# Products without a reader in TensorE's two waits ahead of the expert stage of a hybrid decoder layer

## The reference

```
h = RMSNorm(x + mixers(x))                      # two token mixers ahead of this
g = argmax over 4 groups of h @ w_router_group + b
e1, e2 = the two largest of the 8 experts of group g
combine = softmax weight of the group x softmax over the two experts
y = sum over the two experts of (silu(h @ w_gate[e]) * (h @ w_up[e]) * combine) @ w_down[e]
out = RMSNorm(x + mixers(x) + y)
```

## Time and profile before

| | us |
|---|---|
| median of three runs | 734.78 |
| lowest and highest run | 734.08, 737.99 |
| span of the profiled execution, first to last instruction | 733.4 |
| TensorE's mean granted clock in it, share of full speed | 0.950 |

### The profile page before, as it was taken

One profiled execution on the slowest core, in us unless ns is written; L12 is line 12 of the kernel. 1 busy time (PEld: TensorE's weight loads), 2 busy tenths in 40 slices (PEclk: granted clock), 3 DMA queues, 4 the chain that ended last, 5 costly groups with the idle time before them and its releaser, 6 DMA issues.

```text
span 733.4 us, 13507 instructions
## 1 busy us (share of the span) xinstructions
PE 637.2 (87%) x4935; PEld 450.3 (61%) x4935; DVE 281.4 (38%) x1551; ACT 149.3 (20%) x425; POOL 103.4 (14%) x137
## 2 busy tenths in 40 slices
PE   6999999799999989999998999638997995768674
PEld 4888888687888767743535877436653554444431
DVE  3003845988878976400000222535233221110103
ACT  3333323233326222200010000211100110101013
POOL 1456206320100324000000000011100110000001
PEclk9999999999999999999999999858998998999996
DMA  9938997999998999769999699668999999999871
GB/s 308 291 116 296 365 370 251 328 352 381 348 337 311 391 351 363 301 246 349 410 409 360 224 423 388 266 214 311 351 391 402 372 389 397 388 390 416 365 264 61
DMA packets 94901, 242.86 MB, mean 331 GB/s; under 512 B 8834, under 2 KB 54530, under 8 KB 86514
## 3 DMA queue, kind: packets, MB, share of 16 engines
q1 hardware_dynamic: 58050, 193.51, 69.9%
q10 hardware_dynamic: 31200, 31.39, 12.9%
q0 software_dynamic: 5584, 17.08, 6.9%
HBM read 234.88 MB, written 9.11 MB: 333 GB/s over the span
## 4 chain that ended last, share of the span: by engine, by line
PE 65%; DMA 19%; DVE 9%; SPq 3%; issue 2%; ACT 1%; ACTq 0%; DVEq 0%; POOLq 0%
PE zps L913 40%; PE nps L1195 5%; PE nps L1071 4%; DMA ring_all<-in_w_up 3%; DMA headT<-in_w_up 3%; DMA kall<-in_w_up 3%; DVE kall L1385 3%; DMA ring_all<-in_w_ret_o 3%; PE zps L1218 2%; DMA zret<-in_w_up 2%; PE nps L884 2%; DMA hT<-in_w_down 2%; PE zps L884 1%; PE zps L1184 1%; SPq L453 1%
## 5 line engine op out<-in xcount | busy, mean ns | idle before, releaser
L913 PE MATMUL zps<-hT,ring_all 128*128 128x264 f32 x1152 | 273.5, 393 | 1.6 <-DVE hT L1564 1.0
L913 PEld LDWEIGHTS zps<-hT,ring_all 128*128 128x128 f32 x1152 | 217.6, 193 | 44.9 <-issue 4.2
L1385 DVE CUSTOM_DVE_ANT_0 kall<-kall,qb 128x128 f32<-128x128 f32 x512 | 129.2, 318 | 62.5 <-DMA kall<-in_cache_k 60.0
L606 POOL DMA_INDIRECT rows_b<-h_rows,tidx_i x16 | 15.0, 938 | 343.7 <-DVEq L1652 193.5
L913 PE MATMUL zps<-headT,ring_all 128*128 128x264 f32 x256 | 58.5, 388 | 3.6 <-DMA ring_all<-in_w_ret_o 2.2
L913 PEld LDWEIGHTS zps<-headT,ring_all 128*128 128x128 f32 x256 | 48.2, 190 | 14.7 <-issue 4.8
L1071 PE MATMUL nps<-ring_all,zret 128*64 128x512 f32 x224 | 51.5, 599 | 2.6 <-DMA ring_all<-in_cache_v 2.6
L1726 DVE TENSOR_TENSOR qdT<-qdT,nps 128x64 f32<-128x64 f32 x32 | 7.1, 221 | 101.7 <-ACT qdT L820 101.2
L1385 DVE DVE_READ_ACCUMULATOR2_ANT scores<- 128x1 f32 x512 | 40.5, 79 | 0.0
L1551 DVE TENSOR_TENSOR hT<-zps,zatt 128x264 f32<-128x264 f32 x8 | 3.5, 432 | 92.7 <-PE zps L913 92.6
L820 ACT ACTIVATE qdT<-nps 128x64 f32<-128x64 f32 x32 | 7.1, 223 | 144.5 <-PE nps L1195 144.5
(11 more groups left out here) (374 smaller groups left out, 805.8 us busy)
## 6 DMA issues: line engine op xcount, KB each, us to landing
kall<-in_cache_k SPq DMA_DIRECT2D x64, 512.0 KB, 6.7
ring_all<-in_cache_v SPq DMA_DIRECT2D x56, 512.0 KB, 7.7
ring_all<-in_w_in ACTq DMA_DIRECT2D x26, 1024.0 KB, 9.7
ring_all<-in_w_gate SPq DMA_DIRECT2D x10, 1024.0 KB, 21.5
ring_all<-in_w_up SPq DMA_DIRECT2D x10, 1024.0 KB, 24.4
ring_all<-in_w_down SPq DMA_DIRECT2D x8, 1024.0 KB, 12.7
ring_all<-in_w_in SPq DMA_DIRECT2D x6, 1024.0 KB, 13.4
kall<-in_w_gate SPq DMA_DIRECT2D x5, 1024.0 KB, 16.9
```

The source lines that it names most:

```text
L606: pool.indirect_dma_start(out=rows, out_offset=None, in_=h2_rows, in_offset=bass.IndirectOffsetOnAxis(ap=col, axis=0), bounds_check=T - 1, ...
L913: mm = pe.matmul(zps[m % 2][:, 0:T], w[:, k, P * fb:P * (fb + 1)], rhs[:, k, :], start=(k == 0), stop=(k == KT - 1))
L1385: ins = v.tensor_tensor_reduce(kh, kh, qb[b % 2][:, P * h:P * (h + 1)], 1.0, 0.0, ALU.mult, ALU.add, scores[:, pg, AH * b + h:AH * b + h + 1])
```

## The change

The change adds a helper, `keep_busy(n)`, which issues n products on TensorE: the identity as the stationary tile, the first 384 columns of the constants (identity, ones and an upper triangle) as the moving data, into the first 384 columns of the PSUM bank `zps[1]`. Nobody reads these sums. 24 of them stand between the three transposes of the logits and the wait for `t_oh`, and 12 between the wait for `t_idx` and `pair_x(0)`. Nothing else is changed, and no semaphore is added.

```diff
                 mm = tr(bps[0:r, 512 + 64 * t:512 + 64 * t + G + NE], lgs[:, P * t:P * t + r], G + NE)
             mm.then_inc(t_log, 1)
+
+            def keep_busy(n):
+
+                for _ in range(n):
+                    pe.matmul(zps[1][:, 0:384], ident, cst[:, 0:384], start=True, stop=True, skip_group_check=True)
+
+            keep_busy(24)
             pe.wait_ge(t_oh, 1)
...
             pe.wait_ge(t_idx, 1)
+            keep_busy(12)
             pair_x(0)
             for e in range(NE):
                 expert_gate_up(e)
```

## The result

The changed kernel takes 746.07 us (median of six runs, 743.12 to 749.7) where the kernel before takes 734.87 beside it: 1.0149 times as long, with a 95% interval of 1.0126 to 1.0173. Two later comparisons gave 1.0123 (1.0096 to 1.0150) and 1.0125 (1.0095 to 1.0154). One execution of the first of these, the profiled one, was disturbed (a span of 1318.9 us) and is left out. So the change costs 9 to 11 us. The forecast was 741.0, the range 738.0 to 745.0: right in sign and in the place, too small by 3 to 5 us, and the measured median lies 1.1 us above the range.

What follows compares the result with a forecast made beforehand. Weight transfers were taken to pace the expert stage, so their restart after expert 0's `gate_up` counts. Terms 6.8 - 0.5 - 0.45 + 2.1 - 1.7 = +6.25 us gave 741.0 from 734.78, range 738.0 to 745.0.

Steps and rivals of the forecast that it cites:

- A product of 384 columns: Each added TensorE product at full clock: 0.66 us, by a line between products of 264 and 512 columns.
- The first block: The 24 products ahead of t_oh: 15.8 us in 9.03 us of room, delaying the counting products by 6.8 us.
- The two tables: Counting products and table, between the two blocks: full clock gives back 0.5 and 0.45 us.
- `gate_up` of expert 0: First expert's products behind the gather: at full clock 1.96 us in place of 3.64, giving back 1.7 us.
- the sum: All terms to the end of expert 0's `gate_up`, which frees weight buffers: +6.25 us, bounds +5.15 to +9.9.
- The chain, TensorE's order and the weights that wait for the restart: Expert 0's `gate_up` frees the first weight buffers; added products stand in program order ahead of it, on the chain.
- One for one: From the weights' restart to the end: a late restart is equally late at the end, without room to catch up.
- the term of the 12 others: The 12 products behind t_idx: 7.9 us in a wait of 5.79 us, costing +2.1 us.
- a credit of 0.67: A hole in the weight transfers behind the restart might close: counted as nothing, with 0.67 us as the bound.
- Faster: Rival: both waits hide the products and the clock gains remain; -5.3 us, 729.5, chance 0.04.
- No change: Rival: clock gains run on beyond the restart, at `gate_up` of experts 3 and 5; +2.6 us, 737.4, chance 0.13.
- Much slower: Rival: the clock falls within the added products, being mostly zeros; +31 us, 766, chance 0.05.

Runs made afterwards that it cites:

- e15: The changed kernel repeated without any edit, against the kernel before: ratio 1.0125 (1.0096 to 1.0154 not used; interval 1.0095 to 1.0154), +9.2 us.
- e3: The changed kernel plus two wide products behind the counting products and one behind the small count: ratio 1.0078 to the kernel before, 740.91 us.
- e4: The changed kernel with 13 and 8 wide products for 24 and 12, plus two and one in the small pauses: ratio 1.0027 to the kernel before, 737.75 us.
- e10: Kernel before plus 27 small and 10 wide products, 2 and 1 wide in the pauses, 14 small and 10 wide: ratio 1.0027, +2.0 us.
- e13: Kernel before plus 64 products of 32-column stationary tile and 160 moving columns (32, 5 in the first pause, 27): ratio 0.9993, -0.5 us.
- e7: The changed kernel with 36 small products in place of 8 of the first 24 wide ones: ratio 1.0102 to the kernel before, +7.5 us.
- e9: The changed kernel with 28 more small products ahead of the 24: ratio 1.0169 to the kernel before, +12.4 us.
- e14: The changed kernel's amount of work as 43 and 21 products of 221 columns with a 32-column stationary tile: ratio 1.0104 to the kernel before, +7.6 us.
- e11: Kernel before plus 11 wide, 19 small; 2 wide and 6 small in the pauses; 7 small, 9 wide; 10 small during VectorE's copy: ratio 1.0007, +0.5 us.
- e12: The changed kernel plus 2 wide and 6 small products in the pauses, 10 small ahead of the 12, 10 during VectorE's copy: ratio 1.0117 to the kernel before, +8.6 us.
- e5: The kernel before plus only 24 small products ahead of the wait for t_oh, 96 added instructions: ratio 1.0051, +3.7 us.
- e6: The kernel before plus 40 small products ahead of the wait for t_oh and 24 behind that for t_idx, 256 added instructions: ratio 1.0005, +0.4 us.
- e2: The changed kernel with only the 12 products behind the wait for t_idx, without the first 24: ratio 1.0040 to the kernel before, 737.45 us.

## Why the prediction was wrong

**What held.** A product of 384 columns took 15.68 / 24 = 0.653 us (forecast 0.66). The first block put the counting products 6.5 us later, 488.32 against 480.06 + 1.78 (forecast 6.8). The two tables gave back 1.1 (0.95): `t_idx` came at 491.98 + 0.34 = 492.32, +5.4. `gate_up` of expert 0 gave back 3.64 - 1.96 = 1.7. With these terms the restart was +5.95 in e15 and +5.96 in e3, where the sum said +6.25. The chain, TensorE's order and the weights that wait for the restart are as described. One for one held too: the last weights came 8.77 late for a restart of 8.86, and 6.23 for 5.95 in e15.

**The step that failed first** is the term of the 12 others, and in it the sentence that TensorE would stay at full clock to the end of `gate_up` of expert 0. The 12 were put at 7.9 us and cost +2.1; in the profiled execution they took 10.92, so that the transposes of the rows came 10.57 us late, 5.2 behind `t_idx`. The clock fell at about 491.5, after TensorE had waited 1.4 us for VectorE and made only small products since the counting ones. It is not a fixed cost: e15 had it not, and its term is +2.3. Of the other profiles with both blocks, the clock stayed at 1.00 through the second in e3, e4 and e10, with wide products in both pauses, and in e13, with five of 160 columns in the first; it fell in e7, e9 and e14, with nothing in the pauses, and in e11 and e12, with two wide ones in the first pause and 13 and 16 small ones behind. So wide products in the pauses go with a clock that stays, and quiet pauses mostly, but not always, with one that falls.

**What else was missing** is smaller, and in part open. 3.1 us of the 12, less 0.5 since the first block and the tables came out a little better, make the sum of +6.25 the restart of +8.86. The profiled execution is 745.1 - 733.4 = 11.7 us longer than that of before: 1.78 lie ahead of anything added, 8.77 are the last weights, and 1.15 come behind them. The other profiles have 0.01 to 4.15 us there, so I do not put the 1.78 down to the change. In the later comparisons, at +9, about 3 us were missing, which is what the 12 alone can cost.

Behind the restart I counted nothing, with a credit of 0.67 as the bound, and the 144 instructions I put at nothing without a reason. e5 against e6 shows that added instructions can cost 3.7 us with hardly any work, and the stretch was 1.8 us longer in the changed kernel and 2.85 in e15, with holes that fall where the borders of the instruction packets would. But that these holes made the changed kernel slower is not shown. Its last weights were as late as its restart, so were those of e15, whose profiled execution is 7.0 us longer, 0.87 of it ahead of the change; e2, with a stretch 2.83 longer, has a time of +2.9 for a restart of +2.72; and e14, with the same work and smaller holes, is not measurably faster than e15.

**The rivals.** *Faster* did not come: a product took 0.653 us, over its bounds of 0.376 and 0.48. Nor did e13 gain measurably, where the first block fits its wait and the transposes follow the second without one: the gather waits for the rows in DRAM and the weights for their queue. Products that fit both waits and hold the clock to the end of `gate_up` were not run. *No change* leaned on `gate_up` of experts 3 and 5; e15 still ran the first at 3.39 us. *Much slower* said that the clock falls within the products; it did, but in the second block and not for the zeros that it named, since the same products ran at 1.00 in the first.

## What to carry to other kernels

Products issued to hold the clock stand in order ahead of the ones that are awaited: size them to the shortest wait that they fill, and fill the pauses behind them too, or the clock can fall just where the next block begins. Sized so, they gained nothing measurable here. Look first at what comes next when the chain gets faster; here it was another transfer, 0.7 us away, and a full weight queue behind it. And an edit in a fully unrolled program also moves the borders of the instruction packets of everything behind it: compare the holes without a releaser in both profiles before calling a loss of a few us the work's own, and follow them to the last transfer before calling it theirs.

## What was not expected of the hardware

The same kernel's 12 products took 10.92 us in one execution and 8.01 in another, with the clock at 0.50 and 1.00 over the same stretch. Small products (32 stationary columns, one moving column, 67 ns each at the full clock) count as busy in the profile, yet behind 27 of them in e10, from 472.57 to 474.37, the clock stood at 0.50 from 476 to 478, in the midst of wide products; e9 had the same behind 28. Behind 36 of them in e7 it stayed at 1.00. The wide products that followed, 16 in e7 and 10 in e10:

```profile
474.34 10.59 PE L1149 MATMUL zps<-cst 128*128 128x384 f32 x32
```

```profile
474.37 8.41 PE L1149 MATMUL zps<-cst 128*128 128x384 f32 x20
```

That is 0.66 us each in e7 and 0.84 in e10. Products of the same stationary tile with 160 moving columns ran at a clock of 1.00 over 24.5 us in e13.
